# Element-wise steps of the first layer's two recurrences moved from VectorE to GpSimd

## The chip, the cores and the metric

The kernel runs on one core of a Trainium2 chip, as one program. The metric is the time of one execution on the device, in microseconds; of several runs the median is given. One execution was also taken by the hardware profiler, and its trace is read below. Engines: PE is TensorE (PEld its weight loads), DVE is VectorE, ACT is ScalarE, POOL is GpSimd, SP only issues transfers here. Each engine works through its own list of instructions in order and waits on semaphores for the others.

## The reference

Two layers over 1024 tokens of width 1024, in float32. The first mixes the tokens by two recurrences, then runs a mixture of experts; the second layer (a long convolution, another recurrence and a feed-forward part) isn't touched by the change. The two recurrences of the first layer, cut to what a step over one chunk of tokens computes:

```python
# state-space recurrence, 16 heads of 64, 2 groups, state 128
a_cs = jnp.cumsum(a_c, axis=-1)
seg = jnp.where(mask, a_cs[..., :, None] - a_cs[..., None, :], -jnp.inf)
lmat = jnp.exp(seg)
cb = jnp.einsum('blgn,bsgn->bgls', c_c, b_c)
y = jnp.einsum('bgls,bgrls,bsgrp->blgrp', cb, lmat, x_c)
y = y + jnp.einsum('blgn,bgrpn,bgrl->blgrp', c_c, state, jnp.exp(a_cs))
state = state * jnp.exp(a_cs[..., -1])[..., None, None] + ...
...
y = y.reshape(bsz, seq, SSD_WIDTH) * jax.nn.silu(z.astype(f32))      # output gate of y

# matrix memory, 8 heads of 128
w = jnp.exp(dmat - m_t[..., None])
s = jnp.einsum('blhd,bshd->bhls', q_c, k_c) * w
num = s @ v + (q @ cmem) * inter                                     # written short
h = num / max(|den|, exp(-m_t))                                      # written short
cmem = cmem * carry_scale + ...; nmem = nmem * carry_scale + ...
...
h = jax.nn.sigmoid(o_pre.astype(f32)) * h                            # output gate of mo
```

The reference scans 16 chunks of 64 tokens; the kernel takes 8 of 128, which gives the same sums.

## The kernel before

The kernel is a line of stages in one program, each with its own tiles. `mixers` (lines 829 and following) is the stage that computes both recurrences. It loops over `NCH` = 8 chunks of `CHUNK` = 128 tokens, and every engine has its own list for it, written out by hand; the order in those lists and the semaphores are all that sets the order of the work. `j` is the chunk, `b = j % 2` the half of a double buffer.

SP loads a chunk: `seg` (a row of cumulated decays for each of 16 heads, spread over 128 partitions, 128x2048), `top` (the same for the memory's 8 heads, 128x1024), `qk`, `ch`, `qin` (128x1024) and `vt`, all counted on `loaded[b]`; then `zt` and `ot`, the two gates' factors, on `late[b]`. From the third chunk on the first six wait for `y_done` and `upd` of the chunk that had the buffer, the last two for `gated` and `mo_ok`.

TensorE, per chunk: transposes of `ch` (L970, L977, into `p_c` and `p_a`), `score` (L916), `turn_k` (L921), the product `cb` (L985), the product with `state` (L992, waits for `xdt_ok`), `read(j, 0)` (L932 to L936, waits for `qi_ok`, `cbm_ok`, `ws_ok`), `score`, `update(j, 0)`, `output(j, 0)`, `advance(j, 0)`, then, when `mem_ok` says that the memory of the second half of the heads may be read, `read(j, 1)` (L932 again), `update`, `output` (ends with `y_done`), `advance`, and `read_out(j - 1)`, the transposes of `so` (L903) and `mo` (L909) of the chunk before, which wait for `so_ok` and `mo_ok`.

ScalarE, per chunk: copies `bt`, `weights` (exponentials of `top`, wait for `top_ok`), `decays` (Relu and Exp of `seg`, wait for `seg_ok`), squares, `group_sums(j - 1)` (waits for `gated`), `take_root(j - 1)` (waits for `var_ok`), copies `num`, `scale(j - 1)`, `take(j - 1)`.

VectorE, per chunk: L1185 subtracts the mask from `top`, L1186 subtracts the column table from `seg`, L1190 `xdt` from `p_a`, L1193 multiplies `qin` by the queries, L1145 `weigh`, L1151 `keys`, L1197 `cbm`, `keys`, L1109 the gate of `y` for the chunk before (`out_gate`), L1157 `mask`, L1205 `xdec`, `weigh(j, 1)`, `variance(j - 1)` (L1114 to L1121), L1214 into `y`, `memory(j, 0)` (L1163 to L1168, ends with `mem_ok`), `mask(j, 1)`, `normalise(j - 1)` (L1126 to L1132, the last of them the gate of `mo`), `add_output` (L1173), `states` (L1177, L1180), `memory(j, 1)`, `add_output(j, 1)`, `states(j, 1)`, `take(j - 1)` (L1137, L1139). GpSimd has nothing in this stage. After the loop VectorE does the gate, variance, normalise and take of the last chunk.

Of the kernel before, what the change touches and what calls it, by code (L numbers as in the profile page):

```python
# [21 lines left out]
ALU = mybir.AluOpType  # L22
AXX = mybir.AxisListType.X

P = 128
# [7 lines left out]
CHUNK = 128  # L33
NCH = SEQ // CHUNK
# [38 lines left out]
def past(n):  # L73

    return n + START
# [60 lines left out]
def rows(ap):  # L136

    return ap.rearrange("(t p) n -> p t n", p=P)
# [10 lines left out]
def bc(ap, shape):  # L149
    return ap.to_broadcast(shape)  # L150
# [494 lines left out]
T_DT, T_ACS, T_EA, T_DEC = (SSD_H * n for n in range(4))  # L645
# [4 lines left out]
class GateTables:  # L650
# [4 lines left out]
    H, M = SSD_H, ML_H  # L655
# [173 lines left out]
def mixers(nc, conv, z, vo, gate_rows, gate_ends, tab, d_skip, ident, tri, ones, neg_mask, mixT):  # L829
# [8 lines left out]
    H, G, M, DH = SSD_H, SSD_G, ML_H, ML_D  # L838
    W, NX, HH = SSD_W, SSD_W // P, ML_H // 2
    with Stage(nc, "mix") as s:  # L840
        ch, zt = s.sb("ch", [P, 2, NX + 2 * G, CHUNK]), s.sb("zt", [P, 2, W])
        qk, vt, ot = s.sb("qk", [P, 2, 2 * M, CHUNK]), s.sb("vt", [P, 2, W]), s.sb("ot", [P, 2, W])
        seg, top, qin = (s.sb(n, [P, 2, k, CHUNK]) for n, k in (("seg", H), ("top", M), ("qin", M)))
# [3 lines left out]
        state, y, so = s.sb("state", [P, W]), s.sb("y", [P, 2, W]), s.sb("so", [P, W])  # L847
        kw, mem, nrm = s.sb("kw", [P, M, DH]), s.sb("mem", [P, M, DH]), s.sb("nrm", [P, M])
        num, mo = s.sb("num", [P, 2, W]), s.sb("mo", [P, W])
        var, root, den, ss, eps = s.sb("var", [P, M + G]), s.sb("root", [P, M + G]), s.sb("den", [P, M]), s.sb("ss", [P, M]), s.sb("eps", [P, 1])  # L850
# [3 lines left out]
        c_in, loaded, late = s.sem("c_in"), [s.sem(f"loaded{b}") for b in range(2)], [s.sem(f"late{b}") for b in range(2)]  # L854
        (const_ok, seg_ok, relu_ok, lm_ok, top_ok, wt_ok, qi_ok, bt_turned, bt_ok, x_turned, xdt_ok, xdec_ok, cb_done,
         cbm_ok, scores, ws_ok, kturned, kw_ok, inter, inter_ok, nums, num_ok, upd, mem_ok, mt_ok, y_done, y_ok, st_done,
         st_ok, gated, sq_ok, ssq_ok, var_ok, root_ok, rs_ok, so_ok, mo_ok, so_turned, mo_turned, by_act, by_dve,
         den_ok) = (s.sem(k) for k in (
             "const_ok", "seg_ok", "relu_ok", "lm_ok", "top_ok", "wt_ok", "qi_ok", "bt_turned", "bt_ok", "x_turned",
             "xdt_ok", "xdec_ok", "cb_done", "cbm_ok", "scores", "ws_ok", "kturned", "kw_ok", "inter", "inter_ok", "nums",  # L860
             "num_ok", "upd", "mem_ok", "mt_ok", "y_done", "y_ok", "st_done", "st_ok", "gated", "sq_ok", "ssq_ok", "var_ok",
             "root_ok", "rs_ok", "so_ok", "mo_ok", "so_turned", "mo_turned", "by_act", "by_dve", "den_ok"))
        block = s.block()

        def heads(ap, n):
            return ap.rearrange("p (h q) -> p h q", h=n)

        def each(ap, n, width):
            return bc(ap.unsqueeze(2), [P, n, width])

        def gate(j, at, n):
            return tab[:, j, at:at + n]

        @block.sync
        def _(sp):
            sp.dma_start(dsk[:, :], d_skip.partition_broadcast(P)).then_inc(c_in, 16)
            for el, src in zip((el_a, el_m), gate_ends):
                sp.dma_start(el[:, :, :], src.partition_broadcast(P)).then_inc(c_in, 16)
            for j in range(NCH):
                b, at = j % 2, slice(j * CHUNK, j * CHUNK + CHUNK)  # L880
                if j >= 2:
                    sp.wait_ge(y_done, past(2 * (j - 1)))
                    sp.wait_ge(upd, past(2 * (j - 1)))
                sp.dma_start(seg[:, b], gate_rows[0][j].partition_broadcast(P)).then_inc(loaded[b], 16)
                sp.dma_start(top[:, b], gate_rows[1][j].partition_broadcast(P)).then_inc(loaded[b], 16)
                sp.dma_start(qk[:, b], rows(conv[XBC:, at])).then_inc(loaded[b], 16)
                sp.dma_start(ch[:, b], rows(conv[0:XBC, at])).then_inc(loaded[b], 16)
                sp.dma_start(qin[:, b], gate_rows[2][j].partition_broadcast(P)).then_inc(loaded[b], 16)
                sp.dma_start(vt[:, b], vo[at, 0:W]).then_inc(loaded[b], 16)
                if j >= 2:  # L890
                    sp.wait_ge(gated, past(j - 1))
                    sp.wait_ge(mo_ok, past(j - 1))
                sp.dma_start(zt[:, b], z[at, :]).then_inc(late[b], 16)
                sp.dma_start(ot[:, b], vo[at, W:2 * W]).then_inc(late[b], 16)

        @block.tensor
        def _(pe):
# [198 lines left out]
        def _(v):  # L1096
# [7 lines left out]
                            bc(dsk[:, :].rearrange("p (c a) -> p c a", a=2).unsqueeze(3), [P, NX, 2, 64]),  # L1104
                            ALU.mult).then_inc(const_ok, 1)

            def out_gate(j):
                v.wait_ge(late[j % 2], past(32 * (j // 2 + 1)))
                v.tensor_tensor(y[:, j % 2], y[:, j % 2], zt[:, j % 2], ALU.mult).then_inc(gated, 1)  # L1109

            def variance(j):

                v.wait_ge(sq_ok, past(j + 1))
# [9 lines left out]
            def normalise(j):  # L1123

                v.wait_ge(root_ok, past(j + 1))
                v.reciprocal(root[:, :], root[:, :]).then_inc(rs_ok, 1)  # L1126
                v.drain()
                v.tensor_tensor(den[:, :], den[:, :], root[:, 0:M], ALU.mult)
                v.drain()
                v.tensor_tensor(heads(mo[:, :], M), heads(num[:, j % 2], M), each(den[:, :], M, DH), ALU.mult)  # L1130
                v.drain()
                v.tensor_tensor(mo[:, :], mo[:, :], ot[:, j % 2], ALU.mult).then_inc(mo_ok, 1)  # L1132

            def take(j):
                at = slice(j * CHUNK, j * CHUNK + CHUNK)
# [5 lines left out]
            def weigh(j, f):  # L1141
                o = top[:, j % 2, HH * f:HH * f + HH]
                v.wait_ge(wt_ok, past(2 * j + f + 1))
                v.wait_ge(scores, past(2 * j + f + 1))
                v.tensor_tensor(o, o, heads(p_e[:, :], HH), ALU.mult).then_inc(ws_ok, 1)  # L1145
# [35 lines left out]

            for j in range(NCH):
                b = j % 2
                v.wait_ge(loaded[b], past(96 * (j // 2 + 1)))
                v.tensor_tensor(top[:, b], top[:, b], bc(neg_mask.unsqueeze(1), [P, M, CHUNK]), ALU.subtract).then_inc(top_ok, 1)  # L1185
                v.tensor_tensor(seg[:, b], seg[:, b], each(gate(j, T_ACS, H), H, CHUNK), ALU.subtract).then_inc(seg_ok, 1)  # L1186
                v.wait_ge(x_turned, past(j + 1))
                v.wait_ge(y_done, past(2 * j))
                for g in range(G):
                    last = v.tensor_tensor(heads(xdt[:, g * 512:g * 512 + 512], 8), heads(p_a[g][:, :], 8),  # L1190
                                           each(gate(j, T_DT + 8 * g, 8), 8, 64), ALU.mult)
                last.then_inc(xdt_ok, 1)
                v.tensor_tensor(qin[:, b], qin[:, b], qk[:, b, 0:M], ALU.mult).then_inc(qi_ok, 1)  # L1193
                weigh(j, 0)
                keys(j, 0)
                v.wait_ge(cb_done, past(j + 1))
                v.tensor_tensor(cbm[:, :, :], heads(p_d[:, 0:DEN], G), bc(tri.unsqueeze(1), [P, G, CHUNK]),  # L1197
                                ALU.mult).then_inc(cbm_ok, 1)
                keys(j, 1)
                if j:  # L1200
                    out_gate(j - 1)
                v.drain()
                mask(j, 0)
                v.wait_ge(st_done, past(2 * j))
                v.tensor_tensor(heads(xdec[:, :], H), heads(xdt[:, :], H), each(gate(j, T_DEC, H), H, 64),  # L1205
                                ALU.mult).then_inc(xdec_ok, 1)
                weigh(j, 1)
                if j:
                    variance(j - 1)
                v.wait_ge(inter, past(j + 1))  # L1210
                if j >= 2:
                    v.wait_ge(so_ok, past(j - 1))
                for g in range(G):
                    last = v.tensor_tensor(heads(y[:, b, g * 512:g * 512 + 512], 8), heads(p_a[g][:, :], 8),  # L1214
                                           each(gate(j, T_EA + 8 * g, 8), 8, 64), ALU.mult)
                last.then_inc(inter_ok, 1)
                memory(j, 0)
                mask(j, 1)
                if j:
                    normalise(j - 1)  # L1220
                v.drain()
                add_output(j, 0)
                states(j, 0)
                memory(j, 1)
                v.wait_ge(nums, past(2 * j + 2))
                v.tensor_copy(den[:, :], p_d[:, DEN:DEN + M]).then_inc(den_ok, 1)
                v.drain()
                v.scalar_tensor_tensor(den[:, :], den[:, :], -1.0, den[:, :], ALU.mult, ALU.max)
                add_output(j, 1)
                states(j, 1)  # L1230
                if j:
                    take(j - 1)
                v.drain()
            out_gate(NCH - 1)
            variance(NCH - 1)
            normalise(NCH - 1)
            take(NCH - 1)

# [3104 lines left out]
```

## Time and profile before

| | us |
|---|---|
| median of 3 runs | 4244.78 |
| lowest and highest | 4240.9, 4246.52 |
| the profiled execution's own time | 4246.1 |
| span in its profile | 4244.3 |
| PE busy | 3635.6 (86%) |
| DVE busy | 2833.8 (67%) |
| ACT busy | 1622.2 (38%) |
| POOL busy | 55.9 (1%) |

The stage `mixers` is a small part of the span, some 243 us from 666 to 909 us. The shares of the whole span say little about it; they have to be read for its own stretch. A row of the timeline gives the start in us from the span's start, the duration in us, the engine, the line, the operation with output <- inputs, the shape, and how many in a row are merged; a bracket behind it gives how long its engine had been idle and what released it. `p_a` to `p_g` are PSUM tiles, the others lie in SBUF. SPq rows are the issuing of a transfer; its landing comes later.

### The profile page before, as it was taken

The page shows a single profiled execution, that of the slowest core. Times are in us where ns is not written, and L with a number is a line of the kernel's source. Part 1 is how long each engine was busy: PE and PEld are TensorE (multiplying, and loading weights), DVE is VectorE, ACT ScalarE, POOL GpSimd, SP SyncE. Part 2 cuts the span into 40 slices and gives each one's busy share as a digit, 9 for nine tenths or more (in the row PEclk, how much of TensorE's full clock was granted, in tenths as well). Part 3 has the DMA queues.
Part 4 walks back from the last instruction along what each step waited for, and adds up shares of the span by engine and source line. Part 5 has one row for each costly group of instructions (what it writes and reads, how often), then busy time and mean ns, then how long its engine had stood idle before and what let it go on. Part 6 is the DMA issues. An engine that isn't in the chain of part 4 may idle for free. (4 is left out here: it accounts for less than half of the span.)

```text
span 4244.3 us, 62793 instructions
## 1 busy us (share of the span) xinstructions
PE 3635.6 (86%) x24847; PEld 2938.0 (69%) x24847; DVE 2833.8 (67%) x3475; ACT 1622.2 (38%) x2152; POOL 55.9 (1%) x50
## 2 busy tenths in 40 slices
PE   6999996879849999929999786449998887999898
PEld 4888885767738888817888332229997666888786
DVE  4775326977459999977885688765555547666455
ACT  3222113545337777743333120433332224232244
POOL 0000000000010000010000000000000000000000
PEclk8999998999869999959999898679999898999998
DMA  5942316536489999753332331461110532222565
GB/s 201 334 155 85 113 48 219 199 135 208 138 337 415 413 413 413 323 173 107 100 120 99 122 120 62 144 167 43 43 43 13 168 125 74 81 89 70 185 192 168
DMA packets 300019, 706.20 MB, mean 166 GB/s; under 512 B 55688, under 2 KB 159768, under 8 KB 273530
## 3 DMA queue, kind: packets, MB, share of 16 engines
q1 hardware_dynamic: 264426, 577.64, 38.8%
q10 hardware_dynamic: 20528, 67.11, 4.2%
q0 software_dynamic: 14816, 57.95, 3.8%
q8 instruction: 178, 2.92, 0.3%
q14 instruction: 71, 0.58, 0.0%
HBM read 541.21 MB, written 179.25 MB: 170 GB/s over the span
## 5 line engine op out<-in xcount | busy, mean ns | idle before, releaser
L156 PE MATMUL g_ps<-h1T_hi,g_w_lo 128*128 128x512 f32 x448 | 175.6, 392 | 7.0 <-DVE g_w_lo L355 7.0
L158 PE MATMUL g_ps<-h1T_hi,g_w_hi 128*128 128x512 f32 x448 | 175.0, 391 | 0.0
L157 PE MATMUL g_ps<-h1T_lo,g_w_hi 128*128 128x512 f32 x448 | 175.0, 391 | 0.0
L1784 DVE TENSOR_TENSOR moe_wg_lo<-exp_g,moe_wg_hi 128x2048 fp32r<-128x2048 f32 x68 | 152.8, 2288 | 30.2 <-ACT moe_wg_hi L1738 30.2
L1784 DVE TENSOR_TENSOR moe_wu_lo<-exp_u,moe_wu_hi 128x2048 fp32r<-128x2048 f32 x68 | 152.8, 2288 | 16.3 <-ACT moe_wu_hi L1738 16.3
L4017 DVE TENSOR_TENSOR x3T_lo<-fd_w_raw,x3T_hi 128x1024 fp32r<-128x1024 f32 x66 | 80.8, 1224 | 121.5 <-ACT x3T_hi L3946 121.4
L156 PE MATMUL g_ps<-x2T_hi,g_w_lo 128*128 128x512 f32 x352 | 139.7, 397 | 24.6 <-DVE g_w_lo L582 24.6
L2812 PE MATMUL rs_p_p<-rs_pm,rs_qx 64*64 64x64 f32 x2048 | 157.8, 217 | 2.3 <-issue 2.2
L156 PE MATMUL fd_acc<-x3T_hi,x3T_lo 128*128 128x512 f32 x352 | 139.7, 397 | 19.4 <-DVE x3T_lo L4020 19.4
L156 PE MATMUL g_ps<-g_w_hi,h1T_lo 128*128 128x512 f32 x384 | 149.6, 390 | 0.0
L157 PE MATMUL g_ps<-g_w_lo,h1T_hi 128*128 128x512 f32 x384 | 149.4, 389 | 0.0
L158 PE MATMUL g_ps<-g_w_hi,h1T_hi 128*128 128x512 f32 x384 | 149.4, 389 | 0.0
L1784 DVE TENSOR_TENSOR moe_wd_lo<-exp_d,moe_wd_hi 128x2048 fp32r<-128x2048 f32 x66 | 148.3, 2288 | 1.0
L2812 PEld LDWEIGHTS rs_p_p<-rs_pm,rs_qx 64*64 64x64 f32 x2048 | 143.8, 133 | 0.2 <-issue 0.2
L157 PE MATMUL g_ps<-x2T_lo,g_w_hi 128*128 128x512 f32 x352 | 140.0, 398 | 0.0
L158 PE MATMUL g_ps<-x2T_hi,g_w_hi 128*128 128x512 f32 x352 | 139.8, 397 | 0.0
L157 PE MATMUL fd_acc<-x3T_lo,x3T_hi 128*128 128x512 f32 x352 | 139.1, 395 | 0.0
L158 PE MATMUL fd_acc<-x3T_hi 128*128 128x512 f32 x352 | 139.0, 395 | 0.0
L401 DVE COPY g_st<-g_ps 128x512 f32<-128x512 f32 x24 | 16.6, 691 | 176.4 <-PE g_ps L158 176.4
L2808 PE MATMUL rs_p_q<-rs_qx,rs_pm 64*64 64x128 f32 x1536 | 131.3, 272 | 0.1
L3946 ACT ACTIVATE x3T_hi<-fd_w_raw 128x1024 fp32r<-128x1024 f32 x66 | 70.0, 1060 | 159.5 <-PE fd_acc L158 119.7
L1738 ACT ACTIVATE moe_wg_hi<-exp_g 128x2048 fp32r<-128x2048 f32 x68 | 126.6, 1919 | 0.0
(686 smaller groups left out, 10682.2 us busy)
## 6 DMA issues: line engine op xcount, KB each, us to landing
exp_g<-in_exp_w_gate SPq DMA_DIRECT2D x68, 1024.0 KB
exp_u<-in_exp_w_up SPq DMA_DIRECT2D x68, 1024.0 KB
exp_d<-in_exp_w_down SPq DMA_DIRECT2D x66, 1024.0 KB
fd_w_raw<-in_ffn_w_down SPq DMA_DIRECT2D x66, 512.0 KB, 4.3
go_w_raw<-in_w_out SPq DMA_DIRECT2D x64, 512.0 KB
g_w<-in_w_in SPq DMA_DIRECT2D x52, 512.0 KB, 5.8
g_w<-in_w_in SPq DMA_DIRECT2D x22, 1024.0 KB
moe_x<-s_xs SPq DMA_DIRECT2D x34, 512.0 KB
```

What stands on the lines that cost most here:

```text
L156: pe.matmul(out, l[1], r[0], start=(k == 0), stop=False)
L157: pe.matmul(out, l[0], r[1], start=False, stop=False)
L158: return pe.matmul(out, l[0], r[0], start=False, stop=(k == kt - 1))
L401: v.tensor_copy(st[:, j % 2, 2 * i + 1], ps[:, 2 * i + 1]).then_inc(by_dve, 1)
L1738: act.activation(hi[:, q * m:q * m + m], w[:, q * m:q * m + m], ACT.Copy).then_inc(sem_hi, 1)
L1784: v.tensor_tensor(lo[:, q * m:q * m + m], w[:, q * m:q * m + m], hi[:, q * m:q * m + m], ALU.subtract).then_inc(sem_lo, 1)
L2808: pe.matmul(p_q[g][o, p], pm[o, k], qx[o, k], start=True, stop=True)
L2812: mm = pe.matmul(p_p[g][o, p], q, pm[o, k], start=True, stop=True)
L3946: act.activation(w_hi[:, n % NB], w_raw[:, n % NR], ACT.Copy).then_inc(w_high, 1)
L4017: v.tensor_tensor(w_lo[:, n % NB], w_raw[:, n % NR], w_hi[:, n % NB], ALU.subtract).then_inc(w_low, 1)
```

## The change

GpSimd gets a list of its own in `mixers`. `begin(j)` waits for the chunk's loads and does the two subtractions (`top`, `seg`) and the product `qin`; it is run for chunks 0 and 1 ahead of the loop and for chunk j + 2 within the pass for chunk j. In that pass the gate of `y(j)` comes first, when VectorE has finished both halves of `y` (`y_ok`), then `begin(j + 2)`, then the gate of `mo(j)`, when VectorE has written it (a new semaphore, `raw_ok`). The five instructions leave VectorE's list, with its waits for `loaded` and `late` and one drain. All tiles, buffers, loads and the lists of the other engines stay.

```diff
+        @block.gpsimd
+        def _(pool):
+            def begin(j):
+                b = j % 2
+                pool.wait_ge(loaded[b], past(96 * (j // 2 + 1)))
+                pool.tensor_tensor(top[:, b], top[:, b], bc(neg_mask.unsqueeze(1), [P, M, CHUNK]), ALU.subtract).then_inc(top_ok, 1)
+                pool.tensor_tensor(seg[:, b], seg[:, b], each(gate(j, T_ACS, H), H, CHUNK), ALU.subtract).then_inc(seg_ok, 1)
+                pool.tensor_tensor(qin[:, b], qin[:, b], qk[:, b, 0:M], ALU.mult).then_inc(qi_ok, 1)
+
+            begin(0)
+            begin(1)
+            for j in range(NCH):
+                b = j % 2
+                pool.wait_ge(late[b], past(32 * (j // 2 + 1)))
+                pool.wait_ge(y_ok, past(2 * j + 2))
+                pool.tensor_tensor(y[:, b], y[:, b], zt[:, b], ALU.mult).then_inc(gated, 1)
+                if j + 2 < NCH:
+                    begin(j + 2)
+                pool.wait_ge(raw_ok, past(j + 1))
+                pool.tensor_tensor(mo[:, :], mo[:, :], ot[:, b], ALU.mult).then_inc(mo_ok, 1)
...
-            def out_gate(j):
-                v.wait_ge(late[j % 2], past(32 * (j // 2 + 1)))
-                v.tensor_tensor(y[:, j % 2], y[:, j % 2], zt[:, j % 2], ALU.mult).then_inc(gated, 1)
...
-                v.tensor_tensor(heads(mo[:, :], M), heads(num[:, j % 2], M), each(den[:, :], M, DH), ALU.mult)
-                v.drain()
-                v.tensor_tensor(mo[:, :], mo[:, :], ot[:, j % 2], ALU.mult).then_inc(mo_ok, 1)
+                v.tensor_tensor(heads(mo[:, :], M), heads(num[:, j % 2], M), each(den[:, :], M, DH), ALU.mult).then_inc(raw_ok, 1)
...
-                v.wait_ge(loaded[b], past(96 * (j // 2 + 1)))
-                v.tensor_tensor(top[:, b], top[:, b], bc(neg_mask.unsqueeze(1), [P, M, CHUNK]), ALU.subtract).then_inc(top_ok, 1)
-                v.tensor_tensor(seg[:, b], seg[:, b], each(gate(j, T_ACS, H), H, CHUNK), ALU.subtract).then_inc(seg_ok, 1)
...
-                v.tensor_tensor(qin[:, b], qin[:, b], qk[:, b, 0:M], ALU.mult).then_inc(qi_ok, 1)
...
-                if j:
-                    out_gate(j - 1)
...
-            out_gate(NCH - 1)
```

## Rows read from the trace of the kernel before

**Rows 1.** The page: span, and busy time, share and instructions of each engine.
```profile
span 4244.3 us, 62793 instructions
PE 3635.6 (86%) x24847; PEld 2938.0 (69%) x24847; DVE 2833.8 (67%) x3475; ACT 1622.2 (38%) x2152; POOL 55.9 (1%) x50
```

**Rows 2.** Timelines of chunk 0: VectorE, TensorE and the queue of SP.
```profile
666.50 1.23 DVE L1185 TENSOR_TENSOR mix_top<-mix_top,k_neg 128x1024 f32<-128x1024 f32 x1 [12.14 <-DMA mix_vt<-s_vo]
673.88 0.35 PE L932 MATMUL mix_p_g<-mix_mem,mix_qin 128*128 128x128 f32 x1 [0.57 <-DVE mix_cbm L1197]
675.00 0.44 SPq L889 DMA_DIRECT2D mix_vt<-s_vo  x1
683.75 0.38 PE L932 MATMUL mix_p_g<-mix_mem,mix_qin 128*128 128x128 f32 x2
```

**Rows 3.** Timeline of the stage's end: VectorE, and the next stage's first load.
```profile
899.61 1.23 DVE L1109 TENSOR_TENSOR mix_y<-mix_y,mix_zt 128x1024 f32<-128x1024 f32 x1
909.48 0.33 SPq L3820 DMA_DIRECT2D go_fac<-in_mix_norm  x1
```

**Rows 4.** Table of windows, one steady chunk, with its heading.
```profile
core 0: us, PE busy (x) PEld busy (x) DVE busy (x) ACT busy (x) POOL busy (x), PEclk, DMA share, GB/s
752.78:782.14 29.36, 26.42 (x206) 23.34 (x206) 27.25 (x43) 15.48 (x28) 0.00 (x0) 1.00 0.56 189
```

**Rows 5.** Timeline of TensorE, chunk 4 (782.21 to 811.57).
```profile
786.82 1.98 PE L992 MATMUL mix_p_a<-mix_state,mix_ch 128*128 128x512 f32 x4 [1.35 <-DVE mix_xdt L1190]
789.53 0.46 PE L932 MATMUL mix_p_g<-mix_mem,mix_qin 128*128 128x128 f32 x2 [0.72 <-DVE mix_cbm L1197]
...
799.78 0.49 PE L932 MATMUL mix_p_g<-mix_mem,mix_qin 128*128 128x128 f32 x2 [0.22 <-DVE mix_nrm L1168]
...
809.65 0.60 PE L909 MATMUL mix_p_e<-k_ident,mix_mo 128*128 128x128 f32 x4
...
811.57 1.06 PE L977 MATMUL mix_p_a<-k_ident,mix_ch 128*128 128x128 f32 x8 [0.66 <-DVE mixT L1139]
```

**Rows 6.** Timeline of VectorE, same chunk, not in full.
```profile
782.14 1.23 DVE L1185 TENSOR_TENSOR mix_top<-mix_top,k_neg 128x1024 f32<-128x1024 f32 x1
783.29 2.28 DVE L1186 TENSOR_TENSOR mix_seg<-mix_seg,gate_tab 128x2048 f32<-128x2048 f32 x1
...
786.69 1.21 DVE L1193 TENSOR_TENSOR mix_qin<-mix_qin,mix_qk 128x1024 f32<-128x1024 f32 x1
...
796.08 0.16 DVE L1115 TENSOR_TENSOR mix_den<-mix_den,gate_tab 128x8 f32<-128x8 f32 x1
...
796.59 0.17 DVE L1119 TENSOR_TENSOR mix_ss<-mix_ss,mix_den 128x8 f32<-128x8 f32 x1
796.83 0.17 DVE L1121 TENSOR_TENSOR mix_var<-mix_ss,mix_den 128x8 f32<-128x8 f32 x1
...
799.58 0.15 DVE L1168 TENSOR_TENSOR mix_nrm<-mix_nrm,mix_p_d 128x4 f32<-128x4 f32 x1
...
801.32 1.23 DVE L1130 TENSOR_TENSOR mix_mo<-mix_num,mix_den 128x1024 f32<-128x1024 f32 x1
802.62 1.23 DVE L1132 TENSOR_TENSOR mix_mo<-mix_mo,mix_ot 128x1024 f32<-128x1024 f32 x1
...
804.54 0.68 DVE L1177 TENSOR_TENSOR mix_state<-mix_state,mix_el_a 128x512 f32<-128x512 f32 x1
...
808.10 0.68 DVE L1173 TENSOR_TENSOR mix_y<-mix_y,mix_p_b 128x512 f32<-128x512 f32 x1
```

**Rows 7.** Timeline, GpSimd's only arithmetic on large tiles, and VectorE beside it.
```profile
3258.26 4.43 POOL L3070 TENSOR_SCALAR rw_kT<-rw_kT,rw_cols 128x1024 f32<-128x1024 f32 x4 [1397.39 <-issue]
...
3261.74 1.22 DVE L3049 TENSOR_TENSOR rw_yT<-rw_yT,rf_p_m 128x1024 f32<-128x1024 f32 x1 [3.17 <-PE rf_p_m L3016]
```

**Rows 8.** SP's queue, same chunk; and the tile `vt`: time from issue to landing.
```profile
787.73 0.43 SPq L889 DMA_DIRECT2D mix_vt<-s_vo  x1
...
DMA to landing us min/median/max: 5.4/5.6/7.4
```

More of the change, by code:

```diff
@@ L857, in mixers @@
          st_ok, gated, sq_ok, ssq_ok, var_ok, root_ok, rs_ok, so_ok, mo_ok, so_turned, mo_turned, by_act, by_dve,
-         den_ok) = (s.sem(k) for k in (
+         den_ok, raw_ok) = (s.sem(k) for k in (
              "const_ok", "seg_ok", "relu_ok", "lm_ok", "top_ok", "wt_ok", "qi_ok", "bt_turned", "bt_ok", "x_turned",
@@ L861, in mixers @@
              "num_ok", "upd", "mem_ok", "mt_ok", "y_done", "y_ok", "st_done", "st_ok", "gated", "sq_ok", "ssq_ok", "var_ok",
-             "root_ok", "rs_ok", "so_ok", "mo_ok", "so_turned", "mo_turned", "by_act", "by_dve", "den_ok"))
+             "root_ok", "rs_ok", "so_ok", "mo_ok", "so_turned", "mo_turned", "by_act", "by_dve", "den_ok", "raw_ok"))
         block = s.block()
```

## The prediction

> **What bounds the kernel now.** I read the page first: GpSimd (POOL) is busy 55.9 us of 4244.3 [rows 1], so it has room. The kernel is a line of stages, so what counts is the stage the diff touches, `mixers`. VectorE's timeline starts it at 666.50, when the first wait for `loaded` is over, and the next stage's first load is issued at 909.48, behind its last copy [rows 2, 3]: nothing of the next stage overlaps it, and a us of the stage is a us of the span. The table of windows shows a strict period of 29.36 us per chunk: VectorE busy 27.25, TensorE 26.42, ScalarE 15.48, POOL 0, TensorE's clock 1.00 [rows 4]. Two engines are nearly full. So at most 29.36 - 26.42 = 2.94 us per chunk can come back, whatever leaves VectorE. TensorE's timeline says which part, in the brackets behind its instructions: in a chunk it waits 1.35 us for `xdt` (L1190), 0.72 for `cbm` (L1197), 0.22 for `nrm` (L1168) and 0.66 for the copy L1139 [rows 5].
>
> **What is removed.** Five VectorE instructions per chunk, by their durations: `top` L1185 1.23, `seg` L1186 2.28, `qin` L1193 1.21, gate L1132 1.23 [rows 6], gate L1109 1.23 [rows 3], in all 7.18 us. What TensorE gets: L1185 and L1186 stand ahead of `xdt`, L1193 ahead of `cbm`, so its waits for both go (ScalarE's `weights` then starts as before, behind `bt_ok`, and is early enough). That is 1.35 + 0.72 = 2.07 us. The other two stay. The 0.66 before L977 at 811.57 hangs on VectorE's chain from `y_done` to L1139, which begins with L1173 at 808.10, and in which nothing is removed [rows 5, 6]. The 0.22 hangs on `variance` and `memory(j, 0)`, L1115 at 796.08 to L1168 at 799.58, where nothing is removed either [rows 6]. New period without any cost: 29.36 - 2.07 = 27.29.
>
> **What is added: five POOL instructions.** The only POOL arithmetic on such tiles is L3070, 4.43 us for four of 128x1024, 1.11 each, with one input tensor [rows 7]. The moved ones read two. Bounds: 1.11 per 1024 elements if the second input is free, 2.22 if it costs a pass of its own. Below 1.11 is excluded, the work being no less. I take 2.2, and 4.4 for `seg`, because the row nearest in kind to these has half their inputs. POOL work per chunk: 4 x 2.2 + 4.4 = 13.2 us of 27, so POOL isn't full. What the Trainium skill says of the price (GPSIMD Engine Reference, section 3.1): a tensor_tensor of 2048 fp32 elements takes 4497 ns on GpSimd against 2293 ns on VectorE. The second figure agrees with L1186's 2.28; by the first the sum below would be nearly the same.
>
> **When POOL works.** I count from TensorE's L977, which starts a chunk: 811.57 - 29.36 = 782.21 for the chunk shown [rows 5]. The last load of the next `begin` (`vt`) is issued at 787.73 and lands 5.6 later, at 793.33 [rows 8], which is +11.1. These loads hang on `y_done`, which precedes L977 by 811.57 - 808.10 = 3.5 us, and so keep the offset. `begin(j + 2)` then runs `top` +11.1 to 13.3, `seg` to 17.7, `qin` to 19.9. No one needs its results before the next chunk. The gate of `y` runs early in the chunk, in front of `begin`, and has some 6 us of slack. The gate of `mo` is queued behind `begin(j + 2)` and behind `raw_ok`: free at 19.9, it would end by 22.1; TensorE transposes `mo` at 809.65, +27.4, or +25.4 in the shorter period [rows 5], and SP queues `zt`, `ot` and the next loads behind `mo_ok`, due at `y_done`, +23.8. Cover 1.7 us, so I price that queueing at nothing; if `begin` ran over 1.7 us longer, each us more would be one on the loads. Behind POOL's own waits stand only its later steps: behind `raw_ok` the next gate of `y`, which has its slack, and behind `loaded` the gate of `mo`.
>
> **The unknown that decides: POOL beside VectorE.** While POOL ran L3070, VectorE ran only L3049, which has one SBUF input and one from PSUM, and took its usual 1.22 [rows 7]. No row shows POOL reading beside a VectorE instruction with two inputs in SBUF. Such instructions are a good part of what stays: L1157 x2, L1205, L1130, L1163 x2, L1177 x2 and the 8-column ones L1115, L1119, L1121, L1164. Bounds: they cost nothing more, or each waits until the POOL instruction under way is over. I take the second. It is the harder end of a thing no row decides, and I take it since what would have to be shared is the reading of SBUF by the two engines, and the row that shows them side by side in peace is just the one in which each needs a single SBUF read. In `begin`'s stretch VectorE, 2.07 earlier than shown, wants L1115 at 796.08 - 782.21 - 2.07 = +11.8 [rows 6]. It waits for `top`, +13.3; then L1119 waits for `seg`, +17.7, and L1121 for `qin`, +19.9. From L1121 to the end of L1168 the rows give 799.73 - 796.83 = 2.90, so `mem_ok` comes at +22.8 where it was to come at +15.4: 7.4 us late, and TensorE's `read(j, 1)` at L932 waits for just that, with no cover (its 0.22) [rows 5]. Later L1130 ends 2.8 after `mem_ok`, +25.6; POOL's `mo` gate holds to 27.8 and L1177, due 0.6 behind L1130, waits 1.6; but TensorE needs 8.3 us from L932 at 799.78 to `y_done` and VectorE from L1177 at 804.54 to L1173 at 808.10 only 3.6 [rows 5, 6], so that is covered. Period: 27.29 + 7.4 = 34.7, which is +5.3 per chunk.
>
> The Trainium skill (SBUF — State Buffer, "Who interferes with whom") states that a VectorE instruction with two SBUF inputs contends with a GpSimd instruction that reads SBUF, that the loser blocks for the whole instruction, and that one with a single SBUF input doesn't contend. L3049's 1.22 agrees with the last; nothing in this trace shows the first. By the rule the sum is the one made here, without it that of the first rival.
>
> **The sum, against the profiled run (4246.1; span 4244.3).** Chunk 0: POOL's `top`, `seg`, `qin` run 666.5 to 675.3, and TensorE's first L932, at 673.88, waits for `qi_ok`: +1.4. Then `begin(1)` starts when the second set has landed, 675.00 + 5.6 = 680.6, and holds `nrm` (L1164) until 687.2, so `mem_ok` comes at 688.2, where TensorE's second `read` began at 683.75 [rows 2]: together +4.4. Chunks 1 to 6, each with a `begin` in it: 6 x 5.3 = +31.8. Chunk 7, without one: -2.1. The tail: both gates lie on the chain, the first from 899.61, 2.2 for 1.2 each [rows 3], less what `variance` hides of the first: +1.7. In all +35.8: 4281.9. The three runs' median is 1.3 below the profiled run: 4280.6, rounded 4281.
>
> **Rivals.** (a) No contention, not slower, on the other side. L3049's unchanged 1.22 speaks for it; against it, that the row has no second SBUF read. It decides at `mem_ok`, at +15.4: a `begin` that costs VectorE under 2.07 us there leaves a gain. Chunks 1 to 7: -14.5; chunk 0 +1.4, tail +2.0 (both gates at +1.0). Sum -11.1: 4233.7. With POOL at 1.11 per 1024, chunk 0 gives -2.9 (`qi_ok` at 666.5 + 4.4 = 670.9 against 673.88), the tail -0.2: -17.6, 4227. (b) The two engines share the reads, each slowed: the double of the VectorE rows with two inputs in the stretch (0.16, 0.17, 0.17, 0.15 and L1163, of the shape of L1177, 0.68) is 1.3 us more for 6 chunks, +8 on (a): 4242, no change. (c) Blocking, but POOL at 1.11: `qin` ends at +15.6, `mem_ok` at +18.5, period 30.3, +1.0 for 6 chunks, -2.9 +1 in chunk 0, -2.1 in chunk 7: 4248. (d) The `mo` gate behind `begin`: should `begin` end later than +21.6, loads slip and the loop loads, `begin`, `mo` closes on itself; 2 us for 6 chunks on top of the forecast, 4293, or on (a) 4246.
>
> **How the numbers follow.** A measurement here can tell 0.2%, 8.5 us, from no change. Forecast 0.47, all slower. (a) 0.28: faster 0.21, same 0.07. (b) 0.11: same 0.08, faster 0.02, slower 0.01. (c) 0.08: same 0.07, slower 0.01. (d) 0.06: slower 0.05, same 0.01. Sum: slower 0.54, same 0.23, faster 0.23. The forecast's own range is 4262 (half of the blocking) to 4298. The whole range takes in (a) at POOL's dearer price and (d): 4230 to 4298; (a) at the cheap price and worse pile-ups are left out.
>
> **What would show it.** In the changed trace: POOL's `top` and `seg` durations (2.2 and 4.4, or 1.1 and 2.2); a gap or a stretched duration at L1115, L1119, L1121 while POOL is in `begin`; TensorE's wait at L932 for `nrm` grown from 0.2 to over 7; waits for `xdt` and `cbm` gone; period 34.7 in chunks 1 to 6, 27.3 in chunk 7. The prediction is wrong if that wait stays at 0.2 (then (a)), if VectorE gets ahead of POOL between its instructions each time at small cost, or if `vt` lands so that `begin` misses the stretch from L1115 to L1168.

## The result, and the profile after

The changed kernel takes 4315.9 us (median of 4 runs, 4312.71 to 4320.89), the kernel before 4245.18 beside it. The ratio is 1.0169, 95% interval 1.0152 to 1.0187: slower by 70.7 us, where 36 were forecast and 4298 was the end of the range. The mechanism that was forecast (VectorE's two-input instructions wait for GpSimd's) is in the trace, somewhat smaller than forecast; a second one on top of it (TensorE's clock falls behind the wait), which cost more than twice as much, was not forecast.

The page after, its span and busy times (as [rows 1]):

```profile
span 4310.8 us, 62795 instructions
PE 3689.3 (86%) x24847; PEld 2992.1 (69%) x24847; DVE 2831.2 (66%) x3435; ACT 1621.0 (38%) x2152; POOL 165.4 (4%) x90
```

TensorE does the same 24847 matmuls and is busy 53.7 us longer. VectorE has 40 instructions fewer (8 x 5), some 57 us of work, and is busy only 2.6 us less. Both are signs: neither engine got more work, so some instructions take longer.

The next stage's first load is issued at 984.53 instead of 909.48 [rows 3]: the stage is 75 us longer in the profiled run, and the rest of the kernel 8.5 us shorter, spread over the later stages, which the change doesn't touch; why is open (the four runs of the kernel before lie 5.6 us apart). Windows of the changed kernel, chunk 2 to 4 with their borders from ScalarE's copies of `bt`, and parts of chunk 3 (us, then busy time of PE, PEld, DVE, ACT, POOL, then TensorE's granted clock, share of the DMA engines, GB/s; as [rows 4]):

```profile
738.21:780.00 41.79, 33.89 (x206) 31.02 (x206) 29.32 (x39) 15.37 (x28) 13.25 (x5) 0.75 0.38 126
780.00:822.77 42.77, 35.44 (x206) 32.30 (x206) 28.76 (x39) 15.38 (x28) 13.69 (x5) 0.72 0.43 140
822.77:863.99 41.22, 35.19 (x206) 32.06 (x206) 27.46 (x39) 15.39 (x28) 13.25 (x5) 0.75 0.40 134
...
790.00:795.00 5.00, 5.00 (x41) 4.31 (x39) 4.78 (x7) 2.02 (x5) 2.75 (x2) 1.00 0.07 28
795.00:800.00 5.00, 0.14 (x1) 0.00 (x0) 5.00 (x4) 0.44 (x1) 5.00 (x2) 0.78 0.00 0
800.00:805.00 5.00, 3.19 (x15) 3.19 (x16) 4.67 (x8) 1.33 (x2) 1.25 (x2) 0.50 0.00 0
...
815.00:820.00 5.00, 5.00 (x19) 3.86 (x19) 1.98 (x3) 0.00 (x0) 1.70 (x1) 0.50 0.31 103
820.00:825.00 5.00, 4.34 (x32) 4.13 (x31) 2.16 (x4) 3.29 (x6) 0.98 (x1) 0.83 1.01 316
```

A chunk takes 41 to 43 us instead of 29.36, for the same 206 matmuls. The clock is 1.00 until TensorE stands still at 795, falls while it does, and is 0.50 (1.2 instead of 2.4 GHz) from 800 to beyond 820. In windows of 1 us the low stretch is 797.8 to 821.7; those of the chunks beside it are some 20 us long. The timeline of the three engines in that chunk, in order of time (start, duration, engine, line, operation; as [rows 5, 6]; lines have moved: L1115 to L1121 are now L1132 to L1138, L1163 to L1168 L1178 to L1183, L932 L953, L961 L982, L977 L998):

```profile
780.35 1.06 PE L998 MATMUL mix_p_a<-k_ident,mix_ch 128*128 128x128 f32 x8 [0.66 <-DVE mixT L1154]
...
792.25 2.35 POOL L901 TENSOR_TENSOR mix_top<-mix_top,k_neg 128x1024 f32<-128x1024 f32 x1 [12.49 <-DMA mix_vt<-s_vo]
792.40 2.22 DVE L1138 TENSOR_TENSOR mix_var<-mix_ss,mix_den 128x8 f32<-128x8 f32 x1
794.06 1.08 PE L982 MATMUL mix_p_c<-mix_xdec,mix_bt 128*128 128x512 f32 x2
794.54 1.27 DVE L1223 TENSOR_TENSOR mix_y<-mix_p_a,gate_tab 128x512 f32<-128x512 f32 x2
794.56 3.61 POOL L902 TENSOR_TENSOR mix_seg<-mix_seg,gate_tab 128x2048 f32<-128x2048 f32 x1
795.74 2.97 DVE L1178 TENSOR_TENSOR mix_mem<-mix_mem,mix_el_m 128x512 f32<-128x512 f32 x1
798.12 2.79 POOL L903 TENSOR_TENSOR mix_qin<-mix_qin,mix_qk 128x1024 f32<-128x1024 f32 x1
798.63 2.29 DVE L1179 TENSOR_TENSOR mix_nrm<-mix_nrm,mix_el_m 128x4 f32<-128x4 f32 x1
801.81 0.80 PE L953 MATMUL mix_p_g<-mix_mem,mix_qin 128*128 128x128 f32 x2 [6.68 <-DVE mix_nrm L1183]
804.66 2.36 POOL L915 TENSOR_TENSOR mix_mo<-mix_mo,mix_ot 128x1024 f32<-128x1024 f32 x1 [3.75 <-DVE mix_mo L1147]
805.28 2.28 DVE L1192 TENSOR_TENSOR mix_state<-mix_state,mix_el_a 128x512 f32<-128x512 f32 x1
...
817.23 2.02 PE L982 MATMUL mix_p_c<-mix_xdec,mix_bt 128*128 128x512 f32 x2
...
823.12 1.06 PE L998 MATMUL mix_p_a<-k_ident,mix_ch 128*128 128x128 f32 x8 [0.66 <-DVE mixT L1154]
```

Two things are to be seen. First, VectorE beside POOL: an instruction of 8 columns takes 2.22 us instead of 0.17 and ends with POOL's L901 (794.62 and 794.60). L1178 starts at 795.74, 1.2 us into POOL's L902, and takes 2.97: that instruction ends at 798.17, and 0.54 of L1178's own 0.69 comes behind it. L1179 ends with L903. Between them L1223, which reads PSUM and one SBUF tile, runs right beside L902 in its usual 0.64 each. So instructions with two SBUF inputs stand still until the POOL instruction under way is over, and others don't. It goes the other way too: L903 starts while L1178 has some 0.5 us left to run, and takes 2.79 instead of 2.35. Second, TensorE: the same pair of matmuls L982 takes 1.08 us ahead of the wait and 2.02 behind it.

The chunk can be cut in three at TensorE's wait. Before [rows 5]: 799.78 - 0.22 - 782.21 = 17.35 us from L977's start to the wait, the wait of 0.22, then 811.57 - 799.78 = 11.79 to the next L977. Here: 794.06 + 1.08 - 780.35 = 14.79, a wait of 6.68, then 823.12 - 801.81 = 21.31. The parts: -2.56 (what the freed VectorE gave back), +6.46 (the wait), +9.52 (the low clock); together +13.4. This chunk is the longest of the six; over chunks 1 to 6 the wait was 3.90, 7.25, 6.68, 5.37, 6.57 and 6.51 us, and the mean period 41.7.

### The profile page after: what moved, and what is told of

Same layout as the page of the kernel before. It is cut to its first block and busy times, and to the rows that moved or that the text cites. A ratio compares the mean times of both kernels' runs of the same rounds, so it can differ in the third digit from the quotient of the medians.

```text
span 4310.8 us, 62795 instructions
## 1 busy us (share of the span) xinstructions
PE 3689.3 (86%) x24847; PEld 2992.1 (69%) x24847; DVE 2831.2 (66%) x3435; ACT 1621.0 (38%) x2152; POOL 165.4 (4%) x90
## 3 DMA queue, kind: packets, MB, share of 16 engines
q1 hardware_dynamic: 264426, 577.64, 38.1%
```

## The experiments

**The clock, with GpSimd as it is.**

```diff
                 advance(j, 0)
+                if 1 <= j <= NCH - 2:
+                    pe.wait_ge(ws_ok, past(2 * j + 2))
+                    for _ in range(50):
+                        pe.transpose(p_e[:, 0:128], ident, ident)
                 pe.wait_ge(mem_ok, past(2 * j + 1))
```

> The changed kernel, with 50 spare transposes of the identity (some 5.6 us at TensorE's full clock, into a PSUM bank that nobody reads then) ahead of TensorE's wait for mem_ok in chunks 1 to 6; nothing else. They fill a wait, they compute nothing that is used. Theory A (the wait of 6.7 us lowers TensorE's clock to 0.50 of full, and the slow stretch behind it costs 9.5 us per chunk more): the granted clock stays at 1.00 in chunks 1 to 6, the period falls from 42.8 us to 33.3, which is 6 x 9.5 = 57 us: about 4259. Rival B (the slow matmuls behind the wait have another cause, such as GpSimd's reading): the period stays near 42.8, time 4316 or a little more.

Measured: 4268.39 us (ratio 1.0059, 1.0043 to 1.0076), 47 us faster than the changed kernel with 300 transposes more. Its windows and two rows of its timeline:

```profile
736.00:768.00 32.00, 30.85 (x256) 28.60 (x253) 27.61 (x37) 13.87 (x25) 12.37 (x5) 1.00 0.48 166
768.00:801.00 33.00, 31.75 (x259) 28.87 (x257) 28.27 (x40) 16.11 (x29) 13.92 (x6) 1.00 0.52 169
816.25 5.62 PE L1027 MATMUL mix_p_e<-k_ident 128*128 128x128 f32 x50
821.70 0.39 PE L953 MATMUL mix_p_g<-mix_mem,mix_qin 128*128 128x128 f32 x2
```

The clock stays at 1.00, and the pair at L953 takes 0.39 behind the filled wait where it took 0.80 behind the empty one. The period, as the mean over chunks 1 to 6, falls from 41.7 to 32.9 us (forecast 33.3). B falls. The expected 4259 was 9 us too low. In the profiled run the stage ends at 937.6, 47 us ahead of the changed kernel's 984.53. The six chunks gave 52.7 of the 57, which had been reckoned from chunk 3 alone; but chunk 0, which got no transposes, took 36.4 us instead of 30.3, since its clock fell for some 17 us behind a wait of 1.68 us for `qin`. So 47 us is less than what the clock costs the six chunks.

**The delay, without GpSimd.** In the kernel before, VectorE's first reduction in `variance` is repeated, 6 times, in the short one 2 times.

```diff
                 v.wait_ge(sq_ok, past(j + 1))
+                for _ in range(6 if j <= NCH - 3 else 0):
+                    v.tensor_reduce(ss[:, :], heads(mo[:, :], M), AXX, ALU.add)
+                    v.drain()
                 v.tensor_reduce(ss[:, :], heads(mo[:, :], M), AXX, ALU.add)
```

> The kernel before, GpSimd idle as there, with VectorE's reduction at the head of variance (1.2 us, one SBUF input) repeated six more times in chunks 1 to 6. A pure delay of 7.2 us ahead of mem_ok, without GpSimd. Theory A (TensorE's clock falls for any wait of that length): TensorE waits about 7 us for nrm, the granted clock is 0.50 for some 20 us behind it, period 29.4 + 7.2 + 8 = 44 to 46 us, time 4245 + 6 x 15.5 = 4338. Rival B (the slow stretch belongs to GpSimd's work): the clock stays at 1.00, 6 x 7.2: 4288.

Measured: 4340.18 (1.0227, 1.0209 to 1.0246).

> As the kernel with six repeats, but with two: a delay of 2.4 us. Theory A1 (a wait of 2.4 to 2.6 us on top of the short ones of the chunk is enough to lower the clock, as it was in chunk 1 of the kernel with begin at the border): period 40, time 4305 or more. A2 (such a wait is too short by itself): 6 x 2.4, clock 1.00: 4260.

Measured: 4302.52 (1.0139, 1.012 to 1.0157). The short one's windows and TensorE's two rows around the wait:

```profile
749.92 1.08 PE L961 MATMUL mix_p_c<-mix_xdec,mix_bt 128*128 128x512 f32 x2
753.80 0.49 PE L932 MATMUL mix_p_g<-mix_mem,mix_qin 128*128 128x128 f32 x2 [2.80 <-DVE mix_nrm L1171]
768.66 2.02 PE L961 MATMUL mix_p_c<-mix_xdec,mix_bt 128*128 128x512 f32 x2
...
750.00:755.00 5.00, 2.20 (x12) 1.38 (x11) 4.70 (x13) 0.79 (x2) 0.00 (x0) 0.94 0.00 0
755.00:760.00 5.00, 5.00 (x25) 5.00 (x25) 4.59 (x7) 1.34 (x2) 0.00 (x0) 0.50 0.21 66
```

With GpSimd idle the same thing happens. A wait of 2.80 us at `mem_ok` (0.22 before) is followed by a stretch at 0.50: the waits grew by 6 x 2.58 = 15.5 us, the kernel by 58. With six repeats the wait is 7.97, so 6 x 7.75 = 46.5 us were added to it, and the kernel is 95 longer. So the low clock belongs to the wait, not to GpSimd, and at this place its price, 7.0 and 8.1 us a chunk, hardly depends on the wait's length. (For the short delay the expectation had 4305 or more in the first of its two cases, 2.5 too high.)

**Which of the five.** In one kernel GpSimd does `begin` alone and VectorE both gates, in the other the reverse. POOL's loop of the first, against the changed kernel:

```diff
             begin(0)
             begin(1)
-            for j in range(NCH):
-                b = j % 2
-                pool.wait_ge(late[b], past(32 * (j // 2 + 1)))
+            for j in range(NCH - 2):
                 pool.wait_ge(y_ok, past(2 * j + 2))
-                pool.tensor_tensor(y[:, b], y[:, b], zt[:, b], ALU.mult).then_inc(gated, 1)
-                if j + 2 < NCH:
-                    begin(j + 2)
-                pool.wait_ge(raw_ok, past(j + 1))
-                pool.tensor_tensor(mo[:, :], mo[:, :], ot[:, b], ALU.mult).then_inc(mo_ok, 1)
+                begin(j + 2)
```

> GpSimd does the chunk's two subtractions and the query product at the same places as in the changed kernel; both output gates are back on VectorE. Theory A (all of the loss comes from these three beside variance and memory): about as slow as the changed kernel, 4310 to 4316, period 42 to 43 us, TensorE's wait for nrm over 6 us. Rival C (the gates, at the chunk's start and behind raw_ok, do a good part of the harm): at most 4290.

> GpSimd does only the two output gates; the subtractions and the query product are back on VectorE. Theory A: the mo gate blocks only the multiplication of the state (2.3 instead of 0.7 us), which is covered, the waits of TensorE for xdt and cbm stay as before, the tail is 2 us longer: 4243 to 4249. Rival C: over 4265.

Measured: `begin` alone 4320.24 (1.019, 1.0173 to 1.0207), the gates alone 4247.14 (1.0008, 0.9999 to 1.0018). TensorE in the first:

```profile
801.05 0.80 PE L947 MATMUL mix_p_g<-mix_mem,mix_qin 128*128 128x128 f32 x2 [6.37 <-DVE mix_nrm L1183]
```

The loss is all in `begin` (alone it is even some 4 us above the upper end that was expected, 4316; why is open); C falls. With the gates alone, as expected, a steady chunk keeps its waits of 1.35 and 0.72 us and its 29.36 us. Its chunk 1 took 33.9 us instead of 28.5 though, which was not expected: the waits of 2.34 us for `xdt` and 0.19 for `cbm` there were followed by a low clock too.

**What it stands beside.** The gate of `mo` goes ahead of `begin(j + 2)`:

```diff
-                if j + 2 < NCH:
-                    begin(j + 2)
                 pool.wait_ge(raw_ok, past(j + 1))
                 pool.tensor_tensor(mo[:, :], mo[:, :], ot[:, b], ALU.mult).then_inc(mo_ok, 1)
+                if j + 2 < NCH:
+                    begin(j + 2)
```

> As the changed kernel, but GpSimd does the gate of mo ahead of the next-but-one chunk's subtractions and query product, so that these three fall behind mem_ok, from about +21 to +29 us of a chunk of 27. Theory A (what matters is what they stand beside): variance and the first half of memory run free, TensorE's wait for nrm is near 0.2 again, its clock stays high; the three now hold up the second half's state and memory multiplications by 1 to 3 us, at the chunk's end. Period 27.3 to 31: 4232 to 4256. Rival B (any such reading by GpSimd costs the same wherever it stands): over 4290.

Measured: 4275.12 (1.0083, 1.0058 to 1.0108), between both theories. Rows of one chunk, and the clock around its end:

```profile
815.00 0.49 PE L953 MATMUL mix_p_g<-mix_mem,mix_qin 128*128 128x128 f32 x2 [0.21 <-DVE mix_nrm L1183]
823.43 3.56 DVE L1179 TENSOR_TENSOR mix_nrm<-mix_nrm,mix_el_m 128x4 f32<-128x4 f32 x1
830.04 1.08 PE L930 MATMUL mix_p_e<-k_ident,mix_mo 128*128 128x128 f32 x4 [5.01 <-DVE mix_y L1188]
798.55:832.51 33.96, 28.29 (x206) 25.40 (x206) 27.89 (x39) 15.39 (x28) 14.11 (x6) 0.90 0.48 163
...
831.00:834.00 3.00, 2.55 (x13) 2.18 (x12) 1.56 (x3) 1.96 (x3) 1.72 (x1) 0.50 1.15 348
834.00:837.00 3.00, 3.00 (x23) 3.00 (x22) 2.17 (x4) 2.96 (x7) 0.00 (x0) 0.78 1.08 412
```

The wait at `mem_ok` is back at 0.21. The same blocking now hits the second half's `memory` and comes out as 5 us at the transposes of `mo`, which wait for `y_ok`. The place decides, as A says, but this place isn't free: A's price for it, 1 to 3 us, was too low, since several blocked instructions of VectorE stand in a row (L1192, L1178 and L1179 took 2.29, 2.08 and 3.56 us, 6.4 more than beside an idle GpSimd). A's clock was wrong too: it falls behind the wait of 5.01 us, but only for some 7 us (828.5 to 835.3 in windows of 1 us), where it stayed low for 14 to 24 behind the waits at `mem_ok`, shorter ones among them. TensorE is busy 28.29 us for the 206 matmuls that take 26.42 at 1.00 [rows 4], so here the low clock cost some 2 us a chunk instead of 7 to 9. The price thus depends on where the wait stands, and not on its length alone. What of the place decides it, no run here shows.

**Reads or writes.**

```diff
-                pool.tensor_tensor(top[:, b], top[:, b], bc(neg_mask.unsqueeze(1), [P, M, CHUNK]), ALU.subtract).then_inc(top_ok, 1)
-                pool.tensor_tensor(seg[:, b], seg[:, b], each(gate(j, T_ACS, H), H, CHUNK), ALU.subtract).then_inc(seg_ok, 1)
-                pool.tensor_tensor(qin[:, b], qin[:, b], qk[:, b, 0:M], ALU.mult).then_inc(qi_ok, 1)
+                pool.memset(top[:, b], 300.0).then_inc(top_ok, 1)
+                pool.memset(seg[:, b], 0.0).then_inc(seg_ok, 1)
+                pool.memset(qin[:, b], 0.0).then_inc(qi_ok, 1)
```

> The changed kernel, but GpSimd's three instructions of begin fill top, seg and qin with a constant instead of computing them (this leaves the two subtractions and the query product out): they write the same tiles and read nothing. Theory A1 (the two engines clash over reading SBUF alone): no VectorE instruction with two SBUF inputs is stretched beside them, TensorE's wait for nrm is near 0.2, clock 1.00, period 27.3 us: 4226 to 4238. Rival A2 (any GpSimd instruction on SBUF holds VectorE's two-input ones up): at 1.2 us per 1024 elements the three end at +15.9, the wait is about 3 us per chunk: 4250 or more.

Measured: 4261.9 (1.0041, 1.0026 to 1.0055), but this time can't be read: what is left out changes the routing of the experts, and they load 72 weight tiles instead of 68 (the count of the transfers into `exp_g`). The stage can be read. It ends at 891.4, 18 us ahead of the kernel before, with a period of 26.8 us. Beside GpSimd's writes:

```profile
784.96 0.95 POOL L901 MEMSET mix_top<- 128x1024 f32 x1 [11.38 <-DMA mix_vt<-s_vo]
785.85 1.80 POOL L902 MEMSET mix_seg<- 128x2048 f32 x1
785.62 0.17 DVE L1138 TENSOR_TENSOR mix_var<-mix_ss,mix_den 128x8 f32<-128x8 f32 x1
786.93 0.68 DVE L1178 TENSOR_TENSOR mix_mem<-mix_mem,mix_el_m 128x512 f32<-128x512 f32 x1
787.53 0.15 DVE L1179 TENSOR_TENSOR mix_nrm<-mix_nrm,mix_el_m 128x4 f32<-128x4 f32 x1
```

The very instructions that stood still run in their own times beside GpSimd's writes: A1. VectorE's instructions with two SBUF inputs clash with what GpSimd reads, not with what it writes.

```diff
+                pool.tensor_scalar(top[:, b], top[:, b], 1.0, None, ALU.mult).then_inc(top_ok, 1)
+                pool.tensor_scalar(seg[:, b], seg[:, b], 1.0, None, ALU.mult).then_inc(seg_ok, 1)
+                pool.tensor_scalar(qin[:, b], qin[:, b], 1.0, None, ALU.mult).then_inc(qi_ok, 1)
```

> The changed kernel, but the three instructions of begin multiply their tile by 1.0 in place (this leaves the two subtractions and the query product out): one input read, one output. If one input costs what the kernel before showed (1.11 us per 1024 elements), the three take 4.5 us instead of 8.3. Theory A: VectorE's two-input instructions wait for them still, TensorE's wait for nrm is 2.5 to 3.5 us; with a clock that stays high 4245 to 4252, with one that falls after so short a wait 4290 to 4305. Rival (only GpSimd instructions with two inputs clash): no stretched instruction, 4226 to 4238.

Measured: 4305.74 (1.0142, 1.0122 to 1.0162), again with 72 tiles; the stage ends at 942.5, 33 us later than before. The premise was wrong: on these tiles a one-input instruction took 2.77, 5.4 and 2.77 us, not 1.1 per 1024 elements, so in three chunks POOL was late for the gate of `mo`, and TensorE waited 3.7 to 4.1 us for that at L930. Its wait for `nrm` was 0.2 to 1.1 us, not 2.5 to 3.5. Of the clash it shows this:

```profile
824.34 5.50 POOL L902 TENSOR_SCALAR mix_seg<-mix_seg 128x2048 f32<-128x2048 f32 x1
824.84 3.30 DVE L1145 TENSOR_TENSOR mix_den<-mix_den,mix_root 128x8 f32<-128x8 f32 x1
828.21 1.23 DVE L1147 TENSOR_TENSOR mix_mo<-mix_num,mix_den 128x1024 f32<-128x1024 f32 x1
```

One input on GpSimd's side is enough to hold VectorE up, but not always, nor to the end: L1145 was through at 828.14, 1.7 us ahead of POOL's end at 829.84, and L1147, with two SBUF inputs as well, then ran in its usual 1.23 beside the same L902. Why stays open, and so does the reason for the longer durations. The question on the clock behind so short a wait at `mem_ok`, which the expectation also asked, this run doesn't answer.

**`begin` at the chunk's border.** At a chunk's border VectorE runs copies and products out of PSUM for some 7 us; `begin` is put beside them:

```diff
             begin(0)
-            begin(1)
             for j in range(NCH):
                 b = j % 2
                 pool.wait_ge(late[b], past(32 * (j // 2 + 1)))
                 pool.wait_ge(y_ok, past(2 * j + 2))
+                if j + 1 < NCH:
+                    begin(j + 1)
                 pool.tensor_tensor(y[:, b], y[:, b], zt[:, b], ALU.mult).then_inc(gated, 1)
-                if j + 2 < NCH:
-                    begin(j + 2)
```

> GpSimd does all five, but begin for a chunk stands at that chunk's border (behind y_ok of the chunk before, ahead of its gate of y), where VectorE runs only instructions with a PSUM input for some 7 us (the two copies, xdt, weigh, keys, cbm, keys). Theory A: nothing between weigh(j, 1) and mem_ok is blocked, TensorE's waits for xdt and cbm go, qi_ok comes about 0.9 us late for read(j, 0); tail 2 us longer: period 28.2, time 4235 to 4240. Rival D (the subtractions come too late for ScalarE there, or the gate of y behind them holds up mask and xdec into weigh): 4245 to 4260.

> As the kernel with begin at the chunk's border, but GpSimd does only the two subtractions and the gate of y; the query product and the gate of mo are on VectorE again. Theory A: no late qi_ok, the tail 1 us longer at most; cbm just in time: period 27.3 to 27.8: 4231 to 4236. Rival D: 4245 or more.

Measured: all five at the border 4246.62 (1.0006, 0.9997 to 1.0015), without the query product and the gate of `mo` 4255.43 (1.002, 1.0007 to 1.0034), in runs from 4240.44 to 4271.64. Both expectations (4235 to 4240, 4231 to 4236) missed. The steady chunks of the first do take 28.04 us (28.2 expected), yet its chunk 1 takes 36.2:

```profile
701.95 0.49 PE L952 MATMUL mix_p_g<-mix_mem,mix_qin 128*128 128x128 f32 x2 [2.03 <-POOL mix_qin L903]
...
701.10:704.10 3.00, 2.15 (x19) 2.15 (x20) 2.31 (x2) 3.00 (x7) 3.00 (x2) 1.00 1.16 359
704.10:707.10 3.00, 3.00 (x17) 3.00 (x16) 2.21 (x1) 2.97 (x6) 1.13 (x1) 0.51 0.81 327
```

One wait of 2 us, and one stretch at 0.50 behind it, took back what five chunks had gained. The second kernel had chunks of 38.1, 36.0 and 31.1 us beside 28.3 in its profiled run. It waits 1.30 us for `cbm` in each of chunks 2 to 7, since its VectorE computes the query product ahead of `cbm`, and that product, with two SBUF inputs, stands still beside `begin`:

```profile
790.34 3.61 POOL L902 TENSOR_TENSOR mix_seg<-mix_seg,gate_tab 128x2048 f32<-128x2048 f32 x1
792.67 2.36 DVE L1203 TENSOR_TENSOR mix_qin<-mix_qin,mix_qk 128x1024 f32<-128x1024 f32 x1
```

Behind these equal waits the clock fell in chunks 4, 6 and 7 and stayed at 1.00 in 2, 3 and 5: a wait of this length doesn't decide it alone. The times lie in D's ranges, but not for D's reasons. Both came about in the first kernel's steady chunks and cost nothing: ScalarE waited 1.0 us for `seg`, and `xdec` took 3.39 us instead of 1.22 beside the gate of `y`, but `mask` ran in its usual 1.23, and `weigh` behind `xdec` still had to wait 0.48 us for TensorE.

**The query product a chunk ahead.** The last pair gives the query product back to VectorE, in the pause it has while it waits for `y_done`, for the next chunk (`begin` is then the two subtractions); the second adds 8 spare transposes ahead of `read(j, 0)`.

```diff
+            def query(j):
+                b = j % 2
+                v.wait_ge(loaded[b], past(96 * (j // 2 + 1)))
+                v.tensor_tensor(qin[:, b], qin[:, b], qk[:, b, 0:M], ALU.mult).then_inc(qi_ok, 1)
+
+            query(0)
...
+                if j + 1 < NCH:
+                    query(j + 1)
                 add_output(j, 1)
```

> As the kernel with begin at the chunk's border, but GpSimd does there only the two subtractions and the gate of y (the gate of mo later, as before), and VectorE does the query product one chunk ahead, in the pause before add_output(j, 1). Theory: qi_ok is no longer late, no VectorE instruction ahead of mem_ok is blocked, so TensorE waits only 0.7 and 0.2 us in a chunk, and with so little waiting its clock doesn't fall in chunk 1 either: period 27.3, tail 1 us longer: 4230 to 4236. If the clock still falls in a chunk or two: 4240 to 4250.

> As the kernel with the query product a chunk ahead, with 8 spare transposes (0.9 us) on TensorE ahead of read(j, 0), where the wait for qi_ok and cbm_ok stands, from chunk 1 on. If the clock fell there, it doesn't now: 4233 to 4240. If it didn't fall anyway, the transposes cost up to 0.9 us a chunk: 4236 to 4242.

Measured: 4230.94 (0.9969, 0.9958 to 0.998) and 4234.34 (0.9979, 0.997 to 0.9988). TensorE in the first, with all its waits of a chunk, and two windows:

```profile
762.27 0.49 PE L951 MATMUL mix_p_g<-mix_mem,mix_qin 128*128 128x128 f32 x2 [0.22 <-DVE mix_nrm L1181]
772.50 0.63 PE L928 MATMUL mix_p_e<-k_ident,mix_mo 128*128 128x128 f32 x4 [0.19 <-DVE mix_y L1186]
773.87 0.41 PE L989 MATMUL mix_p_c<-k_ident,mix_ch 128*128 128x128 f32 x2 [0.30 <-DVE mix_state L1193]
775.07 1.06 PE L996 MATMUL mix_p_a<-k_ident,mix_ch 128*128 128x128 f32 x8 [0.79 <-DVE mixT L1152]
...
694.00:722.00 28.00, 26.53 (x210) 23.59 (x210) 23.27 (x41) 15.72 (x28) 12.14 (x5) 1.00 0.67 218
722.00:750.00 28.00, 26.50 (x210) 23.57 (x210) 23.19 (x40) 15.61 (x27) 11.14 (x5) 1.00 0.61 201
```

The waits for `xdt` and `cbm` are gone and no others of their size have come, the clock is 1.00 in chunk 1 too, the mean period is 27.6 us, and the kernel beats both others, by 0.3% against the one before. The transposes were not needed and cost what they take: a steady chunk is 28.67 us long instead of 27.80.

## Why the prediction was wrong

- **What is removed: right.** The waits for `xdt` and `cbm` went, and TensorE reached its wait 2.56 us earlier (2.07 forecast; the rest is in its busy time up to there, 14.79 us instead of 15.28).
- **POOL's price and place: right.** 2.35, 3.61 and 2.35 us undisturbed against 2.2, 4.4 and 2.2, so 8.3 against 8.8; `seg` was cheaper than the double of `top`. In chunk 3 `begin` started at +11.9 of its chunk against +11.1. The Trainium skill's 4497 ns for 2048 elements (GPSIMD Engine Reference, section 3.1) is above the 3.61 measured here, with one of the operands repeated along the row; the measurement decides.
- **The blocking: right, and now shown.** It was a choice between two bounds in the prediction. The trace, the kernel that only writes, and those that move `begin` show it. Which instructions were hit differs from chunk to chunk: in chunk 3 L1138 (L1121 of before), L1178 and L1179, where L1115, L1119 and L1121 were named, since `begin` started 0.8 us later. TensorE's wait differs with them, from 3.90 to 7.25 us, 6.0 in the mean, where 7.4 on top of 0.22 were forecast. With a full clock the period was 32.9 against the forecast 34.7, so this term alone was too big: 3.7 us a chunk instead of 5.3. The stretch of L1192 (1.6 us, covered) came as forecast. The rule of the Trainium skill (SBUF — State Buffer, "Who interferes with whom") agrees with the trace in the changed kernel. By that rule the second to issue is blocked until the first is over; in the kernel with a one-input GpSimd instruction L1145 got through 1.7 us before the end, and there the measurement decides.
- **The step that failed: "Period: 27.29 + 7.4 = 34.7".** It added the wait and took the 11.8 us of TensorE's work behind it over unchanged. In chunk 3 they took 21.3, because the clock fell to 0.50 behind the wait. The clock stood in no term: it was put at nothing, without a reason. For chunks 1 to 6, +31.8 was summed and +74.8 came (their mean went from 29.2 to 41.7). The kernel with the filled wait takes 8.8 us of each back, and the delays without GpSimd bring 7 to 8 us on top of themselves.
- **The rivals.** (a) and (b) fell with the blocking; (c), blocking with POOL at 1.11 us per 1024 elements, fell with POOL's 2.35. ((c)'s 4248 counts from the profiled run, the others' from the median, 1.3 us lower.) (d), the gate of `mo` behind `begin`, was not seen: it was free by 800.9 and needed from 804.7. A late gate of `mo` did come about in three chunks of the kernel with the one-input instructions. None of them, and no end of the range, had the clock in it, though the trace of before could have warned: in [rows 4] TensorE is at 1.00 while busy 26.42 of 29.36 us, but over the stretch in which it is half idle, in a later stage, the same view of the kernel before gives

```profile
1100.00:1206.00 106.00, 53.03 (x256) 45.70 (x254) 44.34 (x144) 19.96 (x29) 14.15 (x15) 0.68 0.58 221
```

- **Chunk 0 and the ends.** Chunk 0 grew by 3.0 us (4.4 forecast), but by another way, so that the near number is luck: `begin(1)` started at 682.83, when `nrm` was through (682.37), and TensorE's second `read` began at 684.04 with no wait. What it held up was the second half of `state` and of `memory`, and TensorE waited 3.04 us for `state` at the chunk's end, where it had waited 1.32. Chunk 7 and the tail together shrank by 2.0 (0.4 forecast).

## What to carry to other kernels

A wait put on a TensorE that is nearly full can cost its own length and then a stretch at half clock behind it, so the sum needs a term, or a rival, for the work that follows; here 2.4 us of delay per chunk cost 9.6, while a wait of 5 us at another place cost some 2 beyond itself. Work moved to GpSimd cost VectorE nothing beside its instructions that read at most one SBUF tile, and held up those that read two. So choose its place by what VectorE runs at that time, not by GpSimd's idle time. And a freed us was worth something only where the waits that were left were small everywhere: with all five moved the kernel was 71 us slower in one place and not clearly different (+2) in another, and with four of them moved and the query product on VectorE, a chunk ahead, 14 us faster.

## What the runs showed of the hardware

- A VectorE instruction of 8 columns took 2.22 instead of 0.17 us, and one of 4 columns 3.56 instead of 0.15, when a two-input GpSimd instruction was under way: each ended with GpSimd's, so what counts is what is left of that one, not their own size. Beside a GpSimd memset they took 0.17 and 0.15.
- GpSimd's own two-input instructions were stretched less: 2.79 instead of 2.35 us for `qin` in chunk 3, which started while a two-input instruction of VectorE had some 0.5 us left to run.
- TensorE's clock fell to 0.50 behind waits of 7.97, 6.68, 5.01, 2.80 and 2.03 us, behind one of 1.30 in some chunks of one kernel and not in others, and not behind the 1.35, 0.72, 0.66 and 0.22 of the kernel before. It came back some 14 to 24 us later behind the waits at `mem_ok`, and some 7 us later behind the 5.01 at the transposes of `mo`. The kernel in which it fell in some chunks had runs 31 us apart.
- 50 transposes of the identity, back to back for 5.6 us in place of a wait, kept the clock at 1.00.
- A GpSimd one-input instruction took 1.11 us for 128x1024 at L3070 [rows 7] and 2.77 for a tile of the same size here; why is open.
